# Transposed projections with the bias on ScalarE, conv taps dealt by step length, later attention slots, and squares and log-sigmoid moved in layer two

## Chip, cores and metric

The kernel runs on one core of one Trainium2 chip. The metric is the device time of one execution in microseconds (us), as the median of three.

## What is computed

Two transformer layers on 256 tokens of width 2048, all in float32. The first (biases and LayerNorm left out here where the change does not touch them):

```python
proj = x @ w_in + b_in              # 2048 -> 5376
c_val, c_glu, c_gate, q, k, v, a_gate = split(proj)   # 1024 x4, 128, 128, 1024
h = c_val * sigmoid(c_glu)
h = layer_norm(causal_depthwise_conv(h, width=31) + conv_b); y_conv = silu(h) * silu(c_gate)
y_attn = sliding_window_attention_with_sinks(q, k, v) * silu(a_gate)   # 16 heads of 64, 2 KV heads
x = layer_norm(ALPHA * x + concat(y_conv, y_attn) @ w_out + b_out)
```

The second layer mixes a sparse attention (NSA, 8 heads of 128) with a gated linear attention (GLA, 4 heads, values 256 wide), then has a cross attention and a gated feed-forward part:

```python
o_nsa = rms_norm(nsa(...), g_nsa_out)                  # RMS norm of each head's row
log_a = log_sigmoid(a_l @ w_gk2 + b_gk) / 16
o_gla = rms_norm(gla(q_l, k_l, v_l, log_a), g_gla_out) * silu(r_l)
x = x + concat(o_nsa, o_gla) @ w_out_2
```

## The kernel before

The time is set by weights passing through TensorE. All weight matrices are cut into 552 **weight steps** of 256 rows (two k-tiles of 128) by mostly 512 columns. A float32 product is made of three products in the rounded type fp32r: each operand is split into a high part and a low rest, and hi x hi, lo x hi and hi x lo are added up in PSUM. `gemm` (L347, L348, L349) does one step: for each of two k-tiles and each of two token tiles three matmuls, 12 in all, each with a 128x128 block of activations stationary (`aH`, `aL`) and 512 weight columns moving. A PSUM pair therefore holds tokens on its partitions and weight columns along the row.

Weights come in chunks of two steps. SP starts one DMA for each chunk into `raw` (4 buffers). ScalarE (ACT) casts raw to `hi` (L358), VectorE (DVE) subtracts to `lo` (L366), each three steps ahead of the step that TensorE (PE) works on. On DVE this is `keep_up(p)`: at the point p of its program it makes the `lo` of step p+3. So a DVE that is late with its other work makes PE wait for `lo`.

Order of the groups of layer one (steps): cv0 0-7 and cv1 16-23 (conv value), cg0 8-15 and cg1 24-31 (conv gate), q0 32-39, q1 40-47, kv 48-55 (256 columns), ga0 56-63, ga1 64-71 (gate of the conv branch), ag0 72-79, ag1 80-87 (gate of the attention), wo0 to wo3 88-119. Then layer two: ..., lq1 168, lar0 176, lk 184, lv0 192, lv1 200, lr1 208, lr2 216-223 (256 columns), w2o0 224, ... Two PSUM pairs alternate between groups.

The other work is written by hand between the steps of each engine. On DVE, after a group's last step, it is evacuated from PSUM with a bias added: `evac` (L1711) for cv and q, `evac_stage` (L1723) for the gates, `glu` (L1727) for the product. The convolution is 248 **taps** of 128x256 (L1746 the first of a channel tile, L1750 the rest), 4 or 5 to a step from p=20 on, each waiting for the tap four before it. Value, query and gate must lie with channels on partitions, so PE transposes them in 128x128 blocks: `conv_in_T` L756 (2x8), `q_T` L767 (2x8), `gate_T` L829 (4x4), and ACT copies them from PSUM.

Attention of layer one is 16 heads, u=0 to 15. With i counted from step 56, head u has its scores on PE (L789, L790) in slot `score_slot`, at i = 2 + 7u//4; DVE does its softmax there (L1759 to L1763), ACT its exponentials, PE transposes the probabilities three steps later (L798) and multiplies by v five steps later (L809 to L811), DVE normalises at six (L1768 to L1772). The conv's LayerNorm runs at i=20 to 29 among them.

In layer two, i is counted from step 168. Log-sigmoid (ACT: Abs, Exp, Ln, L1461 to L1465) runs at i=27, DVE's scans at 29. The GLA levels run at i=31 to 46 on DVE; among them DVE takes the squares of the NSA rows (L2190, L2191). In lr2, DVE multiplies the NSA rows by their inverse root (L2205), copies the GLA output from PSUM (L2211) and squares it (L1958, L1959); after the last step of lr2 PE transposes the result for w2o0.

Of the kernel before, what the change touches and what calls it, by code (L numbers as in the profile page):

```python
# [75 lines left out]
def stack_kernel(nc, a, out):  # L76
# [48 lines left out]
    for g in groups:  # L125
        for c in range(g["kt"] // CHUNK):
            src = g["w"].rearrange("(k p) n -> p k n", p=P)[
                :, g["k0"] + CHUNK * c:g["k0"] + CHUNK * (c + 1), g["col"]:g["col"] + g["n"]]
            chunks.append(dict(src=src, n=g["n"], k=CHUNK, step=g["s0"] + 2 * c, group=g))
            g.setdefault("c0", len(chunks) - 1)  # L130
# [11 lines left out]
    with ExitStack() as ctx:  # L142
# [36 lines left out]
        cols = const("cols", [P, 165])  # L179
# [49 lines left out]
        def wait_raw(e, chunk, later=None):  # L229
            turns = 0 if later is None else plus(later, 16 * later[1] // (CHUNK // STEP * NRAW))  # L230
            e.wait_ge(s_raw[chunk % NRAW], 16 * (chunk // NRAW + 1) + turns)
# [95 lines left out]

        def gemm(pe, g, j, opH, opL, before=None, later=None):
# [22 lines left out]

        def split_hi(act, s, later=None):
# [7 lines left out]
        def split_lo(dve, s, later=None):  # L360
# [3 lines left out]
            if s >= NSLOT:  # L364
# [4 lines left out]
        bias_groups = ["cv0", "cg0", "cv1", "cg1", "q0", "q1", "kv", "ga0", "ga1", "ag0", "ag1",  # L369
                       "wo0", "wo1", "wo2", "wo3"]  # L370
# [10 lines left out]
        c_h = put("c_h", 128, [P, TT, C])  # L381
# [19 lines left out]
        pe_rows = put("pe_rows", 112.5, [64, P])  # L401
# [6 lines left out]
        PEK, PEV = 101, 133  # L408
# [4 lines left out]
        N_PAR = 16 * (len(row_loads) + 2 + 1 + 1 + 1)  # L413
# [5 lines left out]
        s_ch = sem("conv_input_ready")  # L419
        s_cht = sem("conv_input_transposed")  # L420
        s_pad = sem("conv_input_padded")
        s_hT = sem("conv_input_T_ready")
# [11 lines left out]
        s_gat = sem("gate_transposed")  # L434
        s_gT = sem("gate_T_ready")
# [53 lines left out]
        sc8 = put("sc8", 128, [P, TT, GH, DV])  # L489
        mx2, den2 = st2[:, 0:32].rearrange("p (u t) -> p u t", t=2), st2[:, 32:64].rearrange("p (u t) -> p u t", t=2)  # L490
# [18 lines left out]
        sq_m = put("sq_m", 112, [P, D])  # L509
# [28 lines left out]
        s_ffs = sem("ffn_scale_ready")  # L538
        sq_f = put("sq_f", 136, [P, D])
# [45 lines left out]
        def _(sp):  # L585
            def load(c, src=None, later=None):
                ch = chunks[c]
                if c >= NRAW:
# [3 lines left out]
                    else:  # L592
                        sp.wait_ge(s_lo, old["step"] + 2 + plus_steps(later))
                sp.dma_start(raw[:, c % NRAW, :ch["k"] * ch["n"]].rearrange("p (k n) -> p k n", k=ch["k"]),
                             ch["src"] if src is None else src).then_inc(s_raw[c % NRAW], 16)

            for c, ch in enumerate(chunks[:G["fg0"]["c0"]]):
# [14 lines left out]
                if g is not None and g["name"] in bias_groups and c == (g["c0"] if g["i"] else 3):  # L612
                    i = bias_groups.index(g["name"])
                    if i >= 2 and i < 13:
                        evacuated(sp, G[bias_groups[i - 2]])
                    if i >= 13:
                        sp.wait_ge(bias_used, i - 12)
# [39 lines left out]
        def _(pool):  # L657
# [53 lines left out]
            pool.dma_start(pe_rows[32:64, :], a["pe_v_2"][0]).then_inc(s_par, 16)  # L711
            pool.dma_start(cw_rows[:, :], a["conv_w"][0]).then_inc(s_par, 16)
# [12 lines left out]
        score_slot = {2 + 7 * u // 4: u for u in range(HEADS)}  # L725
# [6 lines left out]
        def _(pe):  # L732
# [7 lines left out]
            def param_columns():  # L740
# [3 lines left out]
                pe.transpose(ps_m[2][:, NCOL:165], pe_rows[:, :], ident[0:64, 0:64]).then_inc(s_cols, 1)  # L744
# [5 lines left out]
            def conv_in_T(j):  # L750
                pe.wait_ge(s_ch, j + 1)
                for c in range(4):
                    if c % 2 == 0 and j == 1:
                        pe.wait_ge(s_hT, c // 2 + 1)
                    for t in range(TT):
                        last = pe.transpose(ps_m[c // 2][:, (c % 2) * T + t * P:(c % 2) * T + (t + 1) * P],  # L756
# [1621 lines left out]
```

## Time and profile before

| | |
|---|---|
| time, median of 3 (lowest, highest) | 1740.74 us (1738.15, 1749.26) |
| the profiled execution | 1737.17 us |
| its span, first to last instruction | 1735.1 us |
| mean granted TensorE clock | 0.988 |
| busy: PE, DVE, ACT | 1652.0 (95%), 1076.1 (62%), 776.1 us (45%) |
| weight loads into PE (overlap PE) | 1363.4 us (79%) |
| DMA | 301.40 MB, mean 174 GB/s |

The profile is of one execution; its time and its span differ by 2.07 us, which lies outside the first and last instruction. Busy times are of one engine over the whole span. The profiler gives a matmul a duration longer than the distance to the next one, since they are pipelined; what a matmul costs is the distance between starts. Rows of a timeline give a start, a duration, the engine, the line, the operation, output and inputs, sizes, a count, and in brackets the idle time before it and what ended it.

### The profile page before, as it was taken

How to read it: one execution, taken by the hardware profiler on the slowest of the kernel's cores; microseconds unless marked ns; L12 is line 12 of the kernel's file. 1: busy time of each engine (PE TensorE's matmuls, PEld its weight loads, DVE VectorE, ACT ScalarE, POOL GpSimd, SP SyncE). 2: the span in 40 equal slices, each digit the busy share in tenths (PEclk: the TensorE clock that was granted, in tenths of full speed). 3: DMA queues.
4: the chain of work that ended last, by engine and by line, in shares of the span. 5: the costliest groups of instructions: out<-in, count | busy, mean ns of one | idle time of the engine just before them, and what ended most of it. 6: DMA issues, size and time to landing. Idle time of an engine off the chain costs nothing.

```text
span 1735.1 us, 21788 instructions
## 1 busy us (share of the span) xinstructions
PE 1652.0 (95%) x7929; PEld 1363.4 (79%) x7929; DVE 1076.1 (62%) x1531; ACT 776.1 (45%) x1025; POOL 18.3 (1%) x46
## 2 busy tenths in 40 slices
PE   7999898998999998999998999999999999999998
PEld 6877677786767887787887788888878888888787
DVE  5699996667755666977556655545454445445453
ACT  4433455533534455434554464444433344444332
POOL 3000000000100000000000000000000000000000
PEclk9999999999999999999999999999999999999999
DMA  7664342564576453336554355555555555555553
GB/s 262 204 242 158 119 150 71 184 207 132 169 234 206 127 169 121 98 122 219 180 175 154 122 172 193 193 189 183 185 192 193 192 192 185 185 191 193 175 192 117
DMA packets 160284, 301.40 MB, mean 174 GB/s; under 512 B 5507, under 2 KB 24737, under 8 KB 159696
## 3 DMA queue, kind: packets, MB, share of 16 engines
q1 hardware_dynamic: 159520, 300.14, 52.1%
q8 instruction: 49, 0.80, 0.2%
q0 software_dynamic: 688, 0.23, 0.1%
q14 instruction: 27, 0.22, 0.0%
HBM read 298.26 MB, written 2.10 MB: 173 GB/s over the span
## 4 chain that ended last, share of the span: by engine, by line
PE 82%; DVE 11%; issue 3%; ACT 2%; DMA 1%; DVEq 0%; SPq 0%; ACTq 0%
PE ps_g L347 25%; PE ps_g L349 25%; PE ps_g L348 25%; DVE cT L1750 3%; DVE lo L366 3%; PE ps_m L279 2%; DMA raw<-in_w_in_dram 1%; ACT hi L358 1%; PE ps_m L1055 0%; PE ps_m L997 0%; PE ps_m L840 0%; PE ps_m L939 0%; PE ps_m L920 0%; PE ps_m L1005 0%; DVE sS L1759 0%
## 5 line engine op out<-in xcount | busy, mean ns | idle before, releaser
L366 DVE TENSOR_TENSOR lo<-raw,hi 128x1024 fp32r<-128x1024 f32 (+3 forms) x552 | 652.3, 1185 | 536.6 <-ACT hi L358 528.1
L358 ACT CAST hi<-raw 128x1024 fp32r<-128x1024 f32 (+3 forms) x552 | 562.3, 1021 | 778.5 <-PE ps_g L349 754.2
L347 PE MATMUL ps_g<-hi,aH 128*128 128x512 f32 (+3 forms) x1696 | 665.2, 392 | 15.2 <-DVE lo L366 10.1
L348 PE MATMUL ps_g<-lo,aH 128*128 128x512 f32 (+3 forms) x1696 | 651.1, 384 | 0.0
L349 PE MATMUL ps_g<-hi,aL 128*128 128x512 f32 (+3 forms) x1696 | 650.8, 384 | 0.0
L347 PEld LDWEIGHTS ps_g<-hi,aH 128*128 128x128 f32 x1696 | 323.8, 191 | 81.8 <-issue 21.8
L349 PEld LDWEIGHTS ps_g<-hi,aL 128*128 128x128 f32 x1696 | 323.1, 191 | 63.0
L348 PEld LDWEIGHTS ps_g<-lo,aH 128*128 128x128 f32 x1696 | 323.6, 191 | 58.4 <-issue 0.5
L347 PE MATMUL ps_g<-hi,guH 128*128 128x512 f32 x352 | 137.2, 390 | 0.0
L349 PE MATMUL ps_g<-hi,guL 128*128 128x512 f32 x352 | 137.0, 389 | 0.0
L348 PE MATMUL ps_g<-lo,guH 128*128 128x512 f32 x352 | 137.0, 389 | 0.0
L1750 DVE SCALAR_TENSOR_TENSOR cT<-hT,convw,cT 128x256 f32<-128x256 f32 x240 | 99.2, 472 | 0.0
L348 PEld LDWEIGHTS ps_g<-lo,guH 128*128 128x128 f32 x352 | 66.1, 188 | 13.7
L347 PEld LDWEIGHTS ps_g<-hi,guH 128*128 128x128 f32 x352 | 66.1, 188 | 13.7
L349 PEld LDWEIGHTS ps_g<-hi,guL 128*128 128x128 f32 x352 | 66.1, 188 | 13.5
L296 ACT ACTIVATE aH<-ps_m,cols 128x256 fp32r<-128x256 f32 x64 | 25.7, 475 | 24.1 <-PE ps_m L279 24.1
L313 DVE SCALAR_TENSOR_TENSOR aL<-ps_m,cols,aH 128x256 fp32r<-128x256 f32 x64 | 27.1, 477 | 10.9 <-ACT aH L296 10.9
L279 PE MATMUL ps_m<-ident,x 128*128 128x128 f32 x128 | 19.9, 292 | 13.1 <-DVE x L1919 7.1
L279 PEld LDWEIGHTS ps_m<-ident,x 128*128 128x128 f32 x128 | 16.5, 150 | 16.9 <-issue 14.2
L2239 DVE TENSOR_TENSOR x<-x,ps_g 128x512 f32<-128x512 f32 x32 | 20.5, 683 | 13.2 <-PE ps_g L349 13.2
L347 PE MATMUL ps_g<-hi,mH 128*128 128x512 f32 x64 | 26.2, 409 | 0.0
L347 PE MATMUL ps_g<-hi,ycH 128*128 128x512 f32 x64 | 25.1, 392 | 0.0
(365 smaller groups left out, 1112.4 us busy)
## 6 DMA issues: line engine op xcount, KB each, us to landing
raw<-in_w_gu_dram SPq DMA_DIRECT2D x88, 1024.0 KB, 5.0
raw<-in_w_in_dram SPq DMA_DIRECT2D x76, 1024.0 KB, 6.0
raw<-in_w_down_dram SPq DMA_DIRECT2D x44, 1024.0 KB, 5.0
raw<-in_w_out_dram SPq DMA_DIRECT2D x32, 1024.0 KB, 5.3
raw<-in_w_ck_dram SPq DMA_DIRECT2D x8, 1024.0 KB, 5.4
raw<-in_w_cv_dram SPq DMA_DIRECT2D x8, 1024.0 KB, 6.6
raw<-in_w_in_dram SPq DMA_DIRECT2D x12, 512.0 KB, 3.7
raw<-in_w_cq_dram SPq DMA_DIRECT2D x4, 1024.0 KB, 5.5
```

The lines of the kernel that those rows point to most:

```text
L279: last = pe.transpose(build_bank(name, u)[:, (2 * k + t) * P:(2 * k + t + 1) * P], src(2 * u + k, t), ident[:])
L296: last = act.activation(dst_k, src_k, ACT.Copy, scale=gain(2 * u + k))
L313: last = dve.scalar_tensor_tensor(out=dst_lo(2 * u + k, 1).rearrange("p k t -> p (k t)"), in0=bank[:, k * T:(k + 1) * T], scalar=gain(2 * ...
L347: pe.matmul(dst, xh, wh, start=first, stop=False)
L348: pe.matmul(dst, xh, wl, start=False, stop=False)
L349: last = pe.matmul(dst, xl, wh, start=False, stop=final)
L358: act.copy(step_view(hi, s), raw_view(s)).then_inc(s_hi, 1)
L366: dve.tensor_tensor(step_view(lo, s), raw_view(s), step_view(hi, s).bitcast(F32), ALU.subtract).then_inc(s_lo, 1)
L1750: dve.scalar_tensor_tensor(out=cT[:, ct, :], in0=src, scalar=w, in1=cT[:, ct, :], op0=ALU.mult, op1=ALU.add).then_inc(s_conv, 1)
L2239: dve.tensor_tensor(c, c, ps_g[pair_of(g)][t][:], ALU.add).then_inc(s_free[pair_of(g)], 1)
```

## The change

Layer one, products: the conv groups are now cm0 to cm3 (steps 0 to 31), each of 256 value and the matching 256 gate columns, loaded by two DMAs of 512 KB a chunk instead of one of 1024. For cm0-3, q0, q1, ga0, ga1 (64 steps) `gemm_T` makes the 128x128 block of weights stationary and 256 token columns of the activations move: 24 matmuls of 256 columns a step in place of 12 of 512. The result has channels on its partitions. The 48 transposes, their copies, `c_h`, and the bias evacuations on DVE of these groups go; ACT takes them from PSUM with a bias of one value for each partition (`columns`, `conv_gate`), and DVE makes the conv's input in two operations (`conv_input`).

Layer one, order: the taps go pair of tiles by pair, from p=9 on 4 a step and 3 at every fourth, 1 a step from p=46 to 55, then 5; the wait is for the tap two before. `k_T` and the slots of all 16 heads come one step later.

Layer two: log-sigmoid's three passes are at i=21, 23 and 26, the scans at 29 and 30. The squares of the NSA rows go from DVE to ACT (16 operations with a summed output, i=32 to 39), with the root at i=47. The squares of the GLA output go to ACT, straight from PSUM, in lr2. The evacuation of lr1 on DVE comes behind the scaling of the NSA rows, and the transposes of the first half of w2o0's input come inside lr2 at j=6, into buffers of their own (`y2H`, `y2L`).

```diff
-    for name, col, n in (("cv0", 0, 512), ("cg0", C, 512), ("cv1", 512, 512), ("cg1", C + 512, 512),
-                         ("q0", 3 * C, 512), ("q1", 3 * C + 512, 512), ("kv", 4 * C, 256),
+    for j in range(4):
+        group(f"cm{j}", w_in, T * j, NG)
+    for name, col, n in (("q0", 3 * C, 512), ("q1", 3 * C + 512, 512), ("kv", 4 * C, 256),
...
+                if "halves" in ch:
+                    for h in range(2):
+                        sp.dma_start(dst[:, :, h * T:(h + 1) * T], ch["halves"][h]).then_inc(s_raw[c % NRAW], 16)
...
+        def gemm_T(pe, g, j, before=None):
...
+            for k in range(STEP):
+                kk = STEP * j + k
+                first, final = kk == 0, kk == g["kt"] - 1
+                for ct in range(n // P):
+                    wh = step_view(hi, s)[:, k * n + ct * P:k * n + (ct + 1) * P]
+                    wl = step_view(lo, s)[:, k * n + ct * P:k * n + (ct + 1) * P]
+                    dst = ps_g[pair_of(g)][ct // 2][:, (ct % 2) * T:(ct % 2 + 1) * T]
+                    pe.matmul(dst, wh, aH[:, kk, :], start=first and ct % 2 == 0, stop=False)
+                    pe.matmul(dst, wh, aL[:, kk, :], start=False, stop=False)
+                    last = pe.matmul(dst, wl, aH[:, kk, :], start=False, stop=final and ct % 2 == 1)
...
-        score_slot = {2 + 7 * u // 4: u for u in range(HEADS)}
+        score_slot = {3 + 7 * u // 4: u for u in range(HEADS)}
...
-                    if g["name"] == "ga0" and j == 1:
+                    if g["name"] == "ga0" and j == 2:
                         k_T()
...
+            def columns(name, dst, func, b):
+                g = G[name]
+                psum_ready(act, g)
+                for ct in range(4):
+                    last = act.activation(dst(ct), ps_g[pair_of(g)][ct // 2][:, (ct % 2) * T:(ct % 2 + 1) * T], func,
+                                          bias=cols[:, b + ct:b + ct + 1])
...
+            def conv_input(j):
...
+                dve.wait_ge(s_stga, j + 1)
+                for c in range(2):
+                    ct = 2 * j + c
+                    dve.scalar_tensor_tensor(out=hT[:, ct, TAPS - 1:], in0=ps_g[pair_of(g)][0][:, c * T:(c + 1) * T],
+                                             scalar=cols[:, BCV + ct:BCV + ct + 1],
...
-                        dve.wait_ge(s_conv, i - 3)
+                        dve.wait_ge(s_conv, i - 1)
...
             def conv_share(p):
-                if p >= 20:
-                    conv(min(4 + p % 2, conv_units - conv_at[0]))
+                kv, rate = G["kv"]["s0"], 0
+                if 9 <= p < kv - 2:
+                    rate = 3 if p % 4 == 0 else 4
+                elif kv - 2 <= p < ga:
+                    rate = 1
+                elif p >= ga:
+                    rate = 5
+                conv(min(rate, conv_units - conv_at[0]))
...
-                    if i == 27:
-                        log_sigmoid()
+                    if i in (21, 23, 26):
+                        log_sigmoid((21, 23, 26).index(i))
+                    if 32 <= i < 40:
+                        nsa_squares(2 * (i - 32))
+                        nsa_squares(2 * (i - 32) + 1)
+                    if i == 47:
+                        root(ss_n)
...
+                    if g["name"] == "lr2" and 2 <= j <= 5:
+                        gla_squares(j - 2)
...
                 if i >= 2:
                     pe.wait_ge(s_goc, i - 1)
+                    pe.wait_ge(s_gsq, i - 1)
...
+                    if here == ("lr2", 6):
+                        build_pe(pe, "y2", y2_src, before_y2, only=range(0, 4))
```

How the instructions stand, first on DVE behind the evacuation of the group before q0's, from p=24 of the kernel before. L366 is one step's `lo`, L1711 the evacuation, L1750 the taps:

```order
L1750 SCALAR_TENSOR_TENSOR cT<-hT,convw,cT 128x256 x5
L366 TENSOR_TENSOR lo<-raw,hi 128x1024
L1711 TENSOR_TENSOR c_h<-ps_g,bias 128x512 x2
L1750 SCALAR_TENSOR_TENSOR cT<-hT,convw,cT 128x256 x4
L366 TENSOR_TENSOR lo<-raw,hi 128x1024
L1750 SCALAR_TENSOR_TENSOR cT<-hT,convw,cT 128x256 x5
```

In the changed kernel the taps begin behind cm0, from p=8 on (L399 is `lo`, L1740 the conv's input, L1761 and L1765 the taps):

```order
L1740 SCALAR_TENSOR_TENSOR hT<-ps_g,cols,stg 128x256 x2
L399 TENSOR_TENSOR lo<-raw,hi 128x1024
L1761 TENSOR_SCALAR cT<-hT,convw,cols 128x256 x2
L1765 SCALAR_TENSOR_TENSOR cT<-hT,convw,cT 128x256 x2
L399 TENSOR_TENSOR lo<-raw,hi 128x1024
L1765 SCALAR_TENSOR_TENSOR cT<-hT,convw,cT 128x256 x4
```

The taps moved 11 steps forward and each step has fewer of them; a pair of 512-wide evacuations became a pair 256 wide.

Second, DVE in lr2 of the kernel before. L1948 evacuates lr1 and lr2, L1905 and L2205 invert the root and scale the NSA rows, L2211 copies the GLA output:

```order
L2162 COPY sT<-ps_m 128x512
L1948 TENSOR_SCALAR rl<-ps_g,stat 128x512 x2
L1905 RECIPROCAL st_134<-st_134 128x16
L2205 TENSOR_TENSOR yn<-yn,st_134 128x2048
L366 TENSOR_TENSOR lo<-raw,hi 128x512 x3
L2211 COPY yg<-ps_m 128x512
...
L1958 TENSOR_TENSOR sc_138<-yg 128x2048
L1959 TENSOR_REDUCE stat<-sc_138 128x8
L1908 TENSOR_SCALAR stat<-stat 128x8
```

The same place in the changed kernel (L1904 and L2192 are root and scaling, L1947 the evacuation, L2204 the copy, L399 `lo`):

```order
L2161 COPY sT<-ps_m 128x512
L1904 RECIPROCAL st_133<-st_133 128x16
L2192 TENSOR_TENSOR yn<-yn,st_133 128x2048
L399 TENSOR_TENSOR lo<-raw,hi 128x512
L1947 TENSOR_SCALAR rl<-ps_g,stat 128x512 x2
L399 TENSOR_TENSOR lo<-raw,hi 128x512 x2
L2204 COPY yg<-ps_m 128x512
...
L2204 COPY yg<-ps_m 128x512
L1907 TENSOR_SCALAR stat<-stat 128x8
```

The root and the scaling moved ahead of the evacuation, one `lo` stands between them, and the two squaring instructions are gone from DVE.

## Rows read from the trace of the kernel before

**Rows 1.** The profile's chain of waits, by engine, shares of the span.
```profile
PE 82%; DVE 11%; issue 3%; ACT 2%; DMA 1%; DVEq 0%; SPq 0%; ACTq 0%
```
**Rows 2.** Windows: us; busy of PE, PEld, DVE, ACT, POOL; granted clock, DMA, GB/s.
```profile
104.99:155.34 50.35, 47.38 (x209) 38.69 (x208) 50.35 (x97) 18.44 (x21) 0.00 (x0) 0.97 0.50 175
155.34:172.50 17.16, 13.42 (x105) 12.51 (x104) 17.16 (x39) 7.75 (x11) 0.00 (x0) 1.00 0.61 214
172.50:262.11 89.61, 81.08 (x380) 62.05 (x380) 85.71 (x199) 46.79 (x91) 0.00 (x0) 0.96 0.42 142
262.11:325.07 62.96, 55.85 (x262) 44.35 (x261) 40.50 (x75) 35.64 (x65) 0.00 (x0) 0.95 0.28 96
...
696.25:757.76 61.51, 58.19 (x315) 49.14 (x314) 55.03 (x72) 23.68 (x25) 0.00 (x0) 1.00 0.33 103
757.76:784.15 26.39, 19.13 (x139) 17.79 (x138) 20.05 (x25) 13.65 (x22) 0.00 (x0) 0.98 0.39 139
```
**Rows 3.** PE timeline: matmuls of 512 columns, then of 256 (group kv).
```profile
41.52 0.39 PE L347 MATMUL ps_g<-hi,aH 128*128 128x512 f32 x1
...
60.11 0.39 PE L348 MATMUL ps_g<-lo,aH 128*128 128x512 f32 x1
...
155.34 0.28 PE L347 MATMUL ps_g<-hi,aH 128*128 128x256 f32 x1
...
159.53 0.28 PE L349 MATMUL ps_g<-hi,aL 128*128 128x256 f32 x1
```
**Rows 4.** DVE timeline: five taps and one `lo`.
```profile
102.09 2.05 DVE L1750 SCALAR_TENSOR_TENSOR cT<-hT,convw,cT 128x256 f32<-128x256 f32 x5
104.07 1.21 DVE L366 TENSOR_TENSOR lo<-raw,hi 128x1024 fp32r<-128x1024 f32 x1
105.21 1.26 DVE L1750 SCALAR_TENSOR_TENSOR cT<-hT,convw,cT 128x256 f32<-128x256 f32 x3
```
**Rows 5.** DMA issues of the first weights: KB each, us from issue to landing.
```profile
raw<-in_w_in_dram SPq DMA_DIRECT2D x76, 1024.0 KB, 6.0
...
raw<-in_w_in_dram SPq DMA_DIRECT2D x12, 512.0 KB, 3.7
```
**Rows 6.** PE timeline: the transposes of the conv's input in q0.
```profile
116.22 1.09 PE L756 MATMUL ps_m<-ident,c_h 128*128 128x128 f32 x8 [2.91 <-DVE c_h L1727]
```
**Rows 7.** DVE by line from 104.99 to 172.50: busy us, mean ns | idle.
```profile
L1711 DVE TENSOR_TENSOR q_sb<-ps_g,bias 128x512 f32<-128x512 f32 x4 | 2.5, 671 | 0.0
```
**Rows 8.** DVE timeline: the `lo` of steps 59 and 79.
```profile
180.10 1.21 DVE L366 TENSOR_TENSOR lo<-raw,hi 128x1024 fp32r<-128x1024 f32 x1
...
264.08 1.22 DVE L366 TENSOR_TENSOR lo<-raw,hi 128x1024 fp32r<-128x1024 f32 x1
```
**Rows 9.** PE timeline, ag0 and ag1: waits in attention.
```profile
278.73 0.41 PE L809 MATMUL ps_m<-v_sb,pT 128*128 128x64 f32 x2 [2.26 <-DVE q_sb L1772]
...
308.54 0.87 PE L798 MATMUL ps_m<-ident,sS 128*128 128x128 f32 x3 [2.60 <-ACT pT L1311]
```
**Rows 10.** PE timeline, lk and lv0: waits for the attention of layer two.
```profile
682.53 0.46 PE L1016 MATMUL ps_m<-vw,pT 128*128 128x128 f32 x2 [1.72 <-DVE yn L2085]
...
688.31 0.46 PE L1016 MATMUL ps_m<-vw,pT 128*128 128x128 f32 x2 [2.12 <-DVE yn L2085]
```
**Rows 11.** DVE timeline, GLA levels: squares of the NSA rows (first half).
```profile
714.03 1.21 DVE L2190 TENSOR_TENSOR stg<-yn 128x1024 f32<-128x1024 f32 x1
715.27 1.22 DVE L2191 TENSOR_REDUCE st<-stg 128x8 f32<-128x1024 f32 x1
```
**Rows 12.** Timelines of DVE and ACT in lr2.
```profile
763.71 0.25 DVE L1905 RECIPROCAL st<-st 128x16 f32<-128x16 f32 x1 [3.65 <-ACT st L1394]
...
777.59 2.29 DVE L1959 TENSOR_REDUCE stat<-sc 128x8 f32<-128x2048 f32 x1
...
760.09 1.49 ACT L1555 ACTIVATE rl<-rl 128x1536 f32<-128x1536 f32 x1 [0.96 <-DVE rl L1948]
```
**Rows 13.** PE timeline: the start of w2o0.
```profile
784.15 0.77 PE L347 MATMUL ps_g<-hi,aH 128*128 128x512 f32 x1 [4.13 <-issue]
```

More of the change, by code:

```diff
@@ L230, in wait_raw @@
             turns = 0 if later is None else plus(later, 16 * later[1] // (CHUNK // STEP * NRAW))
-            e.wait_ge(s_raw[chunk % NRAW], 16 * (chunk // NRAW + 1) + turns)
+            in_halves = sum("halves" in ch for ch in chunks[chunk % NRAW:chunk + 1:NRAW])
+            e.wait_ge(s_raw[chunk % NRAW], 16 * (chunk // NRAW + 1 + in_halves) + turns)
         def step_view(buf, s):
@@ L367, in split_lo @@
                               ALU.subtract).then_inc(s_lo, 1)
-        bias_groups = ["cv0", "cg0", "cv1", "cg1", "q0", "q1", "kv", "ga0", "ga1", "ag0", "ag1",
-                       "wo0", "wo1", "wo2", "wo3"]
+        bias_groups = ["kv", "ag0", "ag1", "wo0", "wo1", "wo2", "wo3"]
         bias_used = sem("output_bias_added")
@@ L1354, in _ @@
                         act.activation(rstd_sb[:], rstd_sb[:], ACT.Sqrt).then_inc(s_lna, 1)
-                    if i == 9:
-                        sigmoid(2, ACT.Silu)
-                    if i in (10, 11):
-                        gate_copy(i - 10)
+                    if i == 8:
+                        columns("ga0", lambda ct: gT[:, ct, :], ACT.Silu, BGA)
                     if i == LNI + 6:
@@ L1365, in _ @@
                         last.then_inc(s_lna, 1)
[L1366 to L1369 removed]
+                    if i == 16:
+                        columns("ga1", lambda ct: gT[:, 4 + ct, :], ACT.Silu, BGA + 4)
                     if i == 25:
[L1371 removed]
+                        silu_gate(0)
                     if i == LNI + 8:
@@ L1855, in _ @@
                 if i == 24:
-                    evac_stage(4, "ag0")
+                    evac_gate(0)
                 if i == LNI + 7:
-                    dve.wait_ge(s_gT, 4)
+                    evacuated(dve, G["ga0"])
+                    evacuated(dve, G["ga1"])
                     dve.wait_ge(s_lna, 3)
@@ L2206, in _ @@
                 [P, TT, QH, DK]), ALU.mult).then_inc(s_y2n, 1)
+            keep_up(G["lr2"]["s0"])
+            g = G["lr1"]
+            psum_ready(dve, g)
+            for t in range(TT):
+                take(g, t, rl[:, t, T:T + NG], 0, NG).then_inc(s_free[pair_of(g)], 1)
+            evacuated(dve, g)
             for i in range(4):
@@ L2225, in _, with y2_lo @@
                 [P, TT, GH, DV]), ALU.mult))
+            def y2_lo(us):
+                build_dve(dve, "y2", y2_hi_at, y2_lo_at,
+                          lambda k: cols[:, GNS:GNS + 1] if k < 8 else cols[:, GGL + k % 2:GGL + k % 2 + 1], only=us)
+            y2_lo(range(0, 4))
+            evac_rows("lr2", lambda t: rl[:, t, 768:])
             dve.wait_ge(s_rl, 1)
```

340 lines of the change are left out of this document (139 added, 201 removed).

## The prediction

> **What bounds the kernel now.** I read the chain of waits first, for which engine the end hangs on; then the windows, to see where TensorE is not the one; then the timelines of PE and DVE at the ends of those windows, for the waits themselves. The chain is 82% PE and 11% DVE [rows 1]: nearly everywhere the pace of matmuls is the time, and there is a stretch in which DVE is. The windows show it: from step 32 to 48 (104.99 to 155.34) and in kv (to 172.50) DVE is busy 50.35 of 50.35 and 17.16 of 17.16 us, PE 47.38 and 13.42 [rows 2]. In ga0 to ag0 (172.50 to 262.11) DVE has 85.71 of 89.61. In 262.11 to 325.07 DVE has only 40.50 of 62.96, yet PE lacks 7.1: there it waits for single results, not for load. The changed kernel can gain only in what PE lacks, and pays wherever PE's own work grows.
>
> The pace: 82 matmuls of 512 columns start between 41.52 and 60.11, 0.2267 us each; in kv 35 intervals take 4.19 us, 0.1197 each [rows 3]. So a plain step is 12 x 0.2268 = 2.72 us, and 24 of 256 columns are 24 x 0.1197 = 2.87. DVE's five taps take 104.07 - 102.09 = 1.98, so 0.396 each, and a `lo` 105.21 less 104.07, so 1.14 (its row shows 1.21 with the overlap) [rows 4]. With 4.5 taps a step DVE needs 1.14 + 1.78 = 2.92 in the before, more than PE's 2.72.
>
> **Terms, part by part** (against the profiled time of 1737.17; span 1735.1 and 2.07 around it).
>
> *Steps 0 to 31.* A step costs 2.87 - 2.72 = +0.15. 32 of them: +4.8. Stationary blocks are now weights, 24 loads a step against 12 before. That a load hides behind 256 columns is what kv shows: 104 loads, 12.51 us of busy time, 0.120 each, in 17.16 us, and the matmuls stay at 0.1197 [rows 2, 3]. The kv group has the same 24 loads a step, with activations in them; a weight block has the same size, so I take 0.1197, with 0 to +0.01 as bounds. The Trainium skill ("TensorE: Matmul & The Clock Gate", section "LDWEIGHTS (loading the stationary operand)") puts a load at the number of its columns over 1.2 ns, 107 ns for 128, an estimate just under the matmul's pace; by this rule the margin is a tenth, and the trace, with loads shown at 0.120, does not contradict it. The same page's "Back-to-back issue gap" gives a gap of N/2.4 + 2.5 ns, by which the 64 steps would cost 24 x 109.2 - 12 x 215.8 = 31 ns each, 2 us in all; the trace says 119.7 and 226.7, and 0.15 a step. The measurement decides.
> The first chunk comes as two DMAs of 512 KB: 3.7 us against 6.0 for one of 1024 [rows 5]; two in parallel share the engines, so I take +0.3 for the start (0 to +1). Later chunks are fetched eight steps ahead at a DMA share of 0.5 [rows 2], so nothing. One transposition block of conv_in goes, like the one at 116.22 with 1.09 us: about -0.9. DVE gets 3 or 4 taps a step, 3.75 on average: 1.14 + 1.49 = 2.63 below 2.87, plus two conv-input operations of tap size (0.8) once in eight steps; PE stays ahead. The tap's wait for the tap two before could stall it: a tap shows 0.41 us and starts 0.396 apart, so the one two before ended 0.38 us earlier; nothing (0 to +0.05 a tap, hidden by the 0.24 that is free). Sum at step 32: +4.2.
>
> *Steps 32 to 55.* They took 67.51 us, bound by DVE: 100% busy, with two evacuation pairs of q (4 x 0.671 less overlap, 2.5) and the gate's (1.2) and the product `glu` [rows 2, 7]. The new order leaves PE as the bound: 16 x 2.87 + 8 steps of kv at 24 x 0.1197/2 = 1.44, 11.5, together 57.5. The wait of 2.91 at L756 [rows 6] and a half-clock spell behind it go (clock 0.97 of 50.35 us: 1.5 us [rows 2]). -10.0, so step 56 begins 5.8 early (-3 to -7: DVE may still be a little late at kv, whose steps are 1.44 long while a `lo` of 0.6 and one tap of 0.4 fit, 1.0).
>
> *Steps 56 to 75.* From the `lo` of step 59 (180.10) to that of 79 (264.08) DVE needs 83.98 us for 20 turns of its program [rows 8]. The first started 7.6 us behind PE's step 56; at the nominal lead it would be 1.3 behind. Of the 6.3 us nothing is left if DVE is on time in kv. The load: 5 taps a step for 4.5, +9 taps, +3.6; four half evacuations of ga (4 x 0.67 less overlap) -2.4, and one softmax fewer before step 76, about -1.4. -0.2, so the stretch stays DVE-bound at about 84, and PE's +2.4 in ga0 and ga1 hides in it (16 x 2.87 + 4 x 2.72 and the attention's small matmuls are some 76). Some idle of DVE behind k_T's later slot, +0.5. Together -6.0 (-3 to -7).
>
> *Steps 76 to 87.* PE waits 2.26 us at L809, the same again 22 us later, and 2.60 at L798 [rows 9], 7.1 in all; the clock's 0.95 of 62.96 us means 3.1 us more at half speed [rows 2]. All three waits are heads whose DVE part stands behind a LayerNorm pass. A slot one step later moves them off those; they may fall on others. One score more comes in here, +0.9. I take -5 (0 to -9), by far the least certain term.
>
> *wo0.* The last head is one step later; its probabilities, its product and the transposes for wo0 come 1.8 later in a chain that PE may cover (0 to +3): +1.8.
>
> *lk and lv0.* The waits of 1.72 and 2.12 [rows 10] stand behind DVE's normalising, which waits for ACT, which was held by three log-sigmoid passes at i=27. Spread over three steps they cost each at most one cast's delay. -3.2 (-1 to -4).
>
> *GLA levels.* The squares take 1.21 + 1.22 us on DVE, twice, 4.9 us [rows 11], in a window where DVE has 55.03 of 61.51 and PE 58.19 [rows 2]. PE can win at most the 3.3 it lacks: -3.1 (-2 to -3.5). On ACT, busy 23.68 in the window, 16 small operations have room.
>
> *lr2 and the start of w2o0.* PE has 19.13 of 26.39 us [rows 2]. DVE waits 3.65 for ACT's root before it scales the NSA rows, because lr1's silu (1.49, behind a table load) stands before it; later it squares the GLA rows (2.29 for the sum, as much for the product) and PE stands still 4.13 before w2o0 [rows 12, 13]. Now the root is early, the squares are gone from DVE and the transposes are inside lr2. Against that, PE's GLA output now also waits for ACT's squares, which queue behind the silu, and behind ACT in turn the casts of steps 222 and on. Without all waits 7.3 us could go; I take -3.2 (0 to -6), nearer to the middle than to either end, since a new wait of the silu's length plus its table, some 2.8, is as likely as not.
>
> Sum: 4.2 - 10.0 - 6.0 - 5.0 + 1.8 - 3.2 - 3.1 - 3.2 = -24.5. The profiled execution would take 1712.7 us; the median shown is 3.57 above the profiled one, so **1716.2 us**.
>
> **Rivals.**
>
> *The waits come back elsewhere* (0.20). PE's single waits in attention and in lr2 are chains through three engines; a moved slot may meet another LayerNorm pass, and the new wait for ACT's squares may cost what the root's wait gave. For it: three waits at three different heads, none of which has the same cause. Against: DVE has 22 us free there. Then steps 76 to 87 and lr2 give 0, steps 56 to 75 give 3, lk 2 and the levels 2: -5.8 - 3 + 1.8 - 2 - 2 = -11, 1730 us.
>
> *All waits go* (0.10). -9 at steps 76 to 87, -6 at lr2, and wo0's +1.8 hidden: -24.5 - 4 - 2.8 - 1.8 = -33, 1708, and as low as 1704 if the clock falls nowhere.
>
> *The loads do not hide* (0.04), the case that ends slower. It is one mechanism: PE's loads of weight blocks in gemm_T. In 104.99 to 155.34 a load shows 38.69 / 208 = 0.186 us [rows 2]. If that were its own cost and not the pace of the matmuls beside it, a step of 24 loads would take 4.46 us in place of 2.87, +1.6; over the 48 steps 0 to 47 that is +76, and +18 in 56 to 75, where PE would pass DVE: about 1816 us. It decides for slower by over 1% (17.4 us) from +42 us on, which is 36 ns for each of 1152 matmuls, a pace of 0.156. The kv rows at 0.1197 with 24 loads a step speak against it plainly.
>
> **How the numbers follow.** Forecast 0.66, rivals 0.20, 0.10, 0.04. About 1% (17.4 us) is what a measurement of this kernel can tell from no change, so faster means below 1723.3, slower above 1758.1. The forecast's own terms add to a spread of some 8 us each way; nine tenths of it lie below 1723.3. With the second rival and none of the first: 0.60 + 0.10 + 0.04 for the first's lower edge = 0.74 faster. Same: the forecast's rest 0.06 and the first rival's 0.16 = 0.22. Slower 0.04. The range reaches down to 1704, the low end of the second rival, and up to 1731, just beyond the first.
>
> **What would show it.** In the changed profile: matmuls of gemm_T 0.120 apart; step 32 about 4 us later than 104.99 and step 56 near 166.7 in place of 172.50, with DVE below 100% between them; a clock of 1.00 in that stretch; the `lo` of step 79 near 252; PE waits of under 3 us in all in steps 76 to 87; w2o0's first matmul 20 to 25 us before 784.15, with PE's idle before it gone; nothing changed after it, since no instruction there moved. Wrong would be: matmuls of gemm_T further apart than 0.13; DVE still full to step 56 with PE waiting for `lo`; or in lr2 PE waiting at the GLA output for ACT as long as it waited before for DVE.

## The result

The changed kernel takes 1733.08 us in the median of 20 runs (1728.81 to 1738.43), the kernel before 1745.46 in 20 runs beside it (1737.07 to 1749.26; the three shown above had a median 4.7 lower). The ratio is 0.9935, interval 0.9922 to 0.9948: 11 us gained, where 24.5 were forecast. The forecast time lies 17 us off and the measured one outside its range. In the second comparison (below) the ratio is 0.9948 (0.9928 to 0.9969).

The profiled execution took 1735.88 us, and the one before 1737.17. This pair alone would say that nearly nothing happened, so it has to be read by stretches. The table gives, for stretches between the first matmuls of two steps, the change against before, in microseconds, raw and with the time lost to a halved clock taken out. That time is the sum over all microseconds of (1 - granted clock), from windows of 1 us: 20.5 us up to the last step in the profile before, 30.7 in that after.

| from step | to | forecast | raw | halved clock taken out |
|---|---|---|---|---|
| start | 32 | +4.2 | +4.5 | +4.5 |
| 32 | 56 | -10.0 | -9.9 | -8.2 |
| 56 | 76 | -6.0 | -6.3 | -4.6 |
| 76 | 88 | -5.0 | +4.0 | +4.0 |
| 88 | 96 | +1.8 | +1.2 | +1.2 |
| 96 | 192 | 0 | +8.2 | -2.0 |
| 192 | 200 | -3.2 | -3.0 | -3.0 |
| 200 | 216 | -3.1 | -3.0 | -3.0 |
| 216 | 232 | -3.2 | -0.6 | -0.6 |
| 232 | 551, the last | 0 | +3.3 | -0.1 |
| sum | | -24.5 | -1.6 | -11.9 |

The first row counts from the start of the trace; 0.4 us of it are a later first matmul. Taking the clock out is a little too kind where PE is not the bound: from step 96 to 120 both profiles take 74.5 us, though the changed kernel lost 1.1 us more there to the clock. The timed runs carry a granted clock too. Span times clock is 1701.5 us in the mean for the changed kernel and 1715.3 for the one before (27 runs, those beside e1 to e4 below), so -13.8; the mean clock is 0.983 against 0.985, which gives about 3 to 4 us back.

Windows of the profile after, steps 32 to 48, kv, 56 to 76, 76 to 84 and 84 to 88; columns as in [rows 2]:

```profile
109.48:155.56 46.08, 46.08 (x386) 46.08 (x385) 41.11 (x76) 17.73 (x22) 0.00 (x0) 1.00 0.57 195
155.56:167.08 11.52, 11.52 (x98) 11.52 (x97) 8.34 (x14) 7.62 (x12) 0.00 (x0) 1.00 0.76 269
167.08:250.43 83.35, 77.41 (x545) 69.23 (x543) 78.92 (x187) 45.09 (x92) 0.00 (x0) 0.98 0.43 140
250.43:292.23 41.80, 39.23 (x194) 30.81 (x193) 28.61 (x57) 22.87 (x40) 0.00 (x0) 1.00 0.21 70
292.23:317.41 25.18, 16.81 (x73) 13.12 (x72) 15.09 (x27) 15.82 (x29) 0.00 (x0) 0.86 0.35 129
```

The first two rows are what was forecast: PE full, DVE 41.11 of 46.08 where it was 50.35 of 50.35, clock 1.00, and 385 loads of weight blocks in 46.08 us, 0.1197 each, no more than the matmuls beside them. Kv is 11.52, forecast 11.5. The fifth row is where the expected gain went: four steps took 25.18 us, PE worked 16.81 of them, the clock was 0.86. The same four took 16.0 before.

PE's waits in those four steps, from the view of waits (in total, times, longest):

```profile
PE ps_m L812 <- ACT pT L1314: 6.6, 1, 6.6
PE ps_m L821 <- DVE q_sb L1787: 1.8, 1, 1.8
```

And who held it up, the timelines of ACT and then DVE (L1314 is the copy of the probabilities, L1353 the LayerNorm's silu, L391 the cast, L1304 the exponentials; L399 is `lo`, L1774 the start of a softmax):

```profile
291.16 1.28 ACT L1353 ACT_TABLE_LOAD   x1
292.45 4.05 ACT L1353 ACTIVATE cT<-cT,cols 128x256 f32<-128x256 f32 x8
296.41 1.97 ACT L391 CAST hi<-raw 128x1024 fp32r<-128x1024 f32 x2
298.40 1.28 ACT L1304 ACT_TABLE_LOAD   x1
300.11 0.40 ACT L1304 ACTIVATE sS<-sS,mx 128x128 f32<-128x128 f32 x1 [0.42 <-DVE mx L1778]
...
301.19 0.45 ACT L1314 COPY pT<-ps_m 128x384 f32<-128x384 f32 x1
...
297.47 1.22 DVE L399 TENSOR_TENSOR lo<-raw,hi 128x1024 fp32r<-128x1024 f32 x1 [6.79 <-ACT hi L391]
298.61 0.55 DVE L1774 SCALAR_TENSOR_TENSOR sS<-ps_m,mask 128x384 f32<-128x384 f32 x1
```

Read it backwards. PE wants, and at 301.79 begins, to transpose head 13's probabilities into a PSUM bank from which ACT must first copy head 12's. That copy (301.19) stands in ACT's program behind head 14's exponentials (300.11), these wait for head 14's softmax on DVE (298.61), that stands behind a `lo` (297.47) which waited 6.79 us for a cast, and the casts stand behind eight silus of the conv's LayerNorm (292.45 to 296.5). No engine is full; the order of three programs makes one chain of 10 us.

The same silus held up such a copy before the change too, at a lower price. The wait of 2.60 us at L798 in [rows 9] is this one. ACT in the kernel before (L1362 the silus, L1301 the exponentials, L1311 the copy):

```profile
300.57 4.04 ACT L1362 ACTIVATE cT<-cT,cols 128x256 f32<-128x256 f32 x8
...
306.86 0.40 ACT L1301 ACTIVATE sS<-sS,mx 128x128 f32<-128x128 f32 x1
...
307.94 0.46 ACT L1311 COPY pT<-ps_m 128x384 f32<-128x384 f32 x1
```

There DVE had finished the softmax (at 303.30) while the silus still ran. With the later slots the softmax itself stands behind the late `lo`, so the chain is longer.

In lr2, PE before w2o0 and DVE ahead of it (L2211 scales the GLA rows, L318 makes the low parts of w2o0's input, `y2`):

```profile
780.26 0.47 PE L358 MATMUL ps_g<-hi,y2H 128*128 128x512 f32 x1 [4.25 <-issue]
...
776.96 2.29 DVE L2211 TENSOR_TENSOR yg<-yg,stat 128x2048 f32<-128x2048 f32 x1
779.28 3.23 DVE L318 SCALAR_TENSOR_TENSOR y2L<-ps_m,cols,y2H 128x256 fp32r<-128x256 f32 x8
```

The wait of [rows 13] is as long as before, 4.25 us for 4.13. PE begins when y2's first low parts are there, and these stand behind a scaling that their matmuls don't need; the profile names no releaser ("issue"), and e7 below tests this.

### The profile page after: what moved, and what is told of

It is laid out like the page before. It is cut to its first block, busy times and chain, and to the rows that moved or that the text cites. A ratio compares the mean times of both kernels' runs of the same rounds, so it can differ in the third digit from the quotient of the medians.

```text
span 1733.9 us, 23281 instructions
## 1 busy us (share of the span) xinstructions
PE 1661.2 (96%) x8649; PEld 1406.2 (81%) x8649; DVE 1060.7 (61%) x1515; ACT 786.5 (45%) x1084; POOL 17.7 (1%) x47
## 4 chain that ended last, share of the span: by engine, by line
PE 86%; DVE 8%; ACT 2%; issue 2%; DMA 1%; DVEq 0%; SPq 0%; ACTq 0%
PE ps_g L358 23%; PE ps_g L360 23%; PE ps_g L359 23%; PE ps_g L380 3%; PE ps_g L382 3%; PE ps_g L381 3%; DVE lo L399 2%; PE ps_m L284 2%; DVE cT L1765 2%; ACT hi L391 1%; DMA raw<-in_w_in_dram 1%; PE ps_m L1046 1%; PE ps_m L988 0%; PE ps_m L841 0%; DVE sS L1774 0%
## 5 line engine op out<-in xcount | busy, mean ns | idle before, releaser
L399 DVE TENSOR_TENSOR lo<-raw,hi 128x1024 fp32r<-128x1024 f32 (+3 forms) x552 | 653.1, 1186 | 552.3 <-ACT hi L391 543.6
L391 ACT CAST hi<-raw 128x1024 fp32r<-128x1024 f32 (+3 forms) x552 | 562.8, 1021 | 760.8 <-PE ps_g L360 650.1
L358 PE MATMUL ps_g<-hi,aH 128*128 128x512 f32 (+3 forms) x1376 | 537.8, 391 | 1.5 <-issue 0.8
L359 PE MATMUL ps_g<-lo,aH 128*128 128x512 f32 (+3 forms) x1376 | 526.3, 382 | 0.0
L360 PE MATMUL ps_g<-hi,aL 128*128 128x512 f32 (+3 forms) x1376 | 526.1, 382 | 0.0
L358 PEld LDWEIGHTS ps_g<-hi,aH 128*128 128x128 f32 x1376 | 263.9, 192 | 53.5 <-issue 6.6
L380 PE MATMUL ps_g<-aH,hi 128*128 128x256 f32 x512 | 147.5, 288 | 3.8 <-DVE lo L399 3.8
L381 PE MATMUL ps_g<-aL,hi 128*128 128x256 f32 x512 | 145.8, 285 | 0.0
L382 PE MATMUL ps_g<-aH,lo 128*128 128x256 f32 x512 | 145.8, 285 | 0.0
L380 PEld LDWEIGHTS ps_g<-aH,hi 128*128 128x128 f32 x512 | 99.3, 194 | 5.2 <-issue 5.2
L1765 DVE SCALAR_TENSOR_TENSOR cT<-hT,convw,cT 128x256 f32<-128x256 f32 x240 | 100.6, 478 | 0.0
L381 PEld LDWEIGHTS ps_g<-aL,hi 128*128 128x128 f32 x512 | 99.3, 194 | 0.0
L382 PEld LDWEIGHTS ps_g<-aH,lo 128*128 128x128 f32 x512 | 99.1, 194 | 0.0
L359 PEld LDWEIGHTS ps_g<-lo,guH 128*128 128x128 f32 x352 | 66.1, 188 | 13.8
```

The costliest lines, as they stand in the source:

```text
L358: pe.matmul(dst, xh, wh, start=first, stop=False)
L359: pe.matmul(dst, xh, wl, start=False, stop=False)
L360: last = pe.matmul(dst, xl, wh, start=False, stop=final)
L380: pe.matmul(dst, wh, aH[:, kk, :], start=first and ct % 2 == 0, stop=False)
L381: pe.matmul(dst, wh, aL[:, kk, :], start=False, stop=False)
L382: last = pe.matmul(dst, wl, aH[:, kk, :], start=False, stop=final and ct % 2 == 1)
```

## The experiments

Times are medians, the ratio is against the kernel before on the same chip. The runs were made in three groups, each on a chip of its own (e1 to e4, e5 to e8, e9 to e11), so the groups are compared with one another and with the result by their ratios: a difference of 0.001 is 1.7 us. Lengths of stretches come from each run's profile, halved clock taken out unless said; times at which a step comes are as in the profile.

**e1, the slots back.**
```diff
-        score_slot = {3 + 7 * u // 4: u for u in range(HEADS)}
+        score_slot = {2 + 7 * u // 4: u for u in range(HEADS)}
```
(and `k_T` at j=1 again)

> The changed kernel with one part undone: the 16 heads' slots (and k_T) one step earlier, as before. In the changed kernel the stretch from step 84 to 88 takes 25.2 us where the kernel before takes 16.0, with PE waiting 6.6 us for a head's exponentials on ScalarE. Theory A (collision): with the later slots a head's exponentials come between the gate's silu at i=25 and the LayerNorm silu at i=26, so ScalarE loads its table four times instead of two and the casts wait behind; slots back to the old place take this away: steps 84 to 88 about 17 us, the time 5 to 8 us below the changed kernel, ratio to before about 0.989. Theory B (the waits come from PE arriving early, whatever the slots): steps 84 to 88 stay at 23 us or more, or the wait turns up two or three steps away, and the time is within 2 us of the changed kernel.

1730.98 us, ratio 0.9921 (0.9900 to 0.9943). Steps 84 to 88 fell from 21.8 to 14.6 us; raw 15.8, near the 17 expected. But by the ratios the time is only some 2 us below the changed kernel's, less than the intervals can tell and not the 5 to 8 expected, since steps 76 to 84 grew from 41.8 to 46.0. The waits from step 76 to 84 are those of the kernel before, 2.3 twice and 2.6:

```profile
PE ps_m L821 <- DVE q_sb L1787: 4.5, 2, 2.3
PE ps_m L812 <- ACT pT L1314: 2.6, 1, 2.6
```

So the collision belongs to the slots (Theory A), and its price was right, but A had missed that the late slots gain about 5 us ahead of it. Both signs are in the one edit.

**e2, the gate's silu beside the LayerNorm's**, to save table loads.
```diff
                     if i == LNI + 6:
+                        silu_gate(0)
...
-                    if i == 25:
-                        silu_gate(0)
```

> The changed kernel with ScalarE's silu of the first attention gate moved from i=25 to i=26, directly ahead of the LayerNorm silu and behind the head's exponentials. The slots stay late. Theory A (table loads on ScalarE): two loads of 1.28 go from the chain, steps 84 to 88 get 2.5 to 4 us shorter than the changed kernel's 25.2. If it is only the eight silu operations (4.05 us) that hold the casts up, not the tables, they stay within 1 us of 25.2. Theory B as for the run with the slots back: no change.

1733.41 us, ratio 0.9939 (0.9908 to 0.9969). Steps 84 to 88 took 22.6 us, 0.8 longer; PE's longest wait was 7.4. ACT where the two loads went:

```profile
291.12 0.40 ACT L1304 ACTIVATE sS<-sS,mx 128x128 f32<-128x128 f32 x1 [3.49 <-DVE mx L1777]
```

Counted from step 80, these exponentials begin 0.8 us earlier than in the changed kernel. The rest of the time that the two loads and the gate's silu took ahead of them is now spent standing still, waiting for DVE's softmax, and the gate's silu (1.06 us) stands in the chain behind them instead. So the two loads that e2 removes are worth 0.8 us, and not the wait of 6.6. Two more stand in the chain itself (at 291.16 and 298.40 in the changed kernel, 1.28 us each); what these cost no run tests.

**e3, the taps dealt as before.**
```diff
-                kv, rate = G["kv"]["s0"], 0
...
-                conv(min(rate, conv_units - conv_at[0]))
+                if p >= 20:
+                    conv(min(4 + p % 2, conv_units - conv_at[0]))
```

> The changed kernel with the conv taps dealt as before: none until p=20, then 4 and 5 in turn, also in the key and value group. Theory A (DVE's load by step length is what steps 56 to 76 gain from): DVE needs 2.92 us a step where PE needs 2.87, and in kv 2.4 where PE needs 1.44, so it enters step 56 some 7 us late; steps 32 to 56 take about 58 to 60 us, but steps 56 to 76 take 83 to 89 us less the taps already done, and step 76 comes 5 to 7 us later than in the changed kernel (250.4). Rival (the gain came from the evacuations and transposes that went, not from the dealing of taps): step 76 within 2 us of 250.4.

1737.88 us, ratio 0.9972 (0.9952 to 0.9992). Step 76 came 7.3 us later than in the changed kernel. The rows of 32 to 56 and 56 to 76:

```profile
109.23:170.96 61.73, 58.44 (x482) 57.74 (x481) 61.73 (x126) 26.35 (x35) 0.00 (x0) 1.00 0.58 196
170.96:257.77 86.81, 78.00 (x542) 69.55 (x543) 81.52 (x191) 44.29 (x92) 0.00 (x0) 0.98 0.43 140
```

DVE is full again to step 56, 61.73 of 61.73, and PE stands still 3.3 us. Step 56 comes 3.9 us later, and from there to step 76 another 3.5 are lost. Dealing is worth 6.0 us at step 96; that is Theory A.

**e4, layer one alone** (the edits of layer two left out).

> The kernel before with the change's first half only: transposed projections, taps and slots in layer one; layer two as before. My account of the two traces, with the time lost to a halved clock taken out of both, gives layer one -4.3 us at step 96 and layer two -7 us (lk to lv1 -6.1, lr2 -0.8). Theory A (the parts add up): ratio to before 0.996 to 0.999, that is -2 to -6 us, and against the changed kernel +6 to +8. Rival (the changed kernel's layer two gains only what the clock did not take, and in the median nothing): this kernel is as fast as the changed one within 2 us.

1737.84 us, ratio 0.9963 (0.9943 to 0.9982). Up to step 192 it is the changed kernel within 0.3 us. From 192 to 200 the changed kernel gains 2.9 us on it and from 200 to 208 another 3.0: log-sigmoid's and the squares' places, as forecast. In the profiles the parts add up. In the time layer two is worth 5 us by the ratios (0.9963 against 0.9935), a little under the 6 to 8 expected.

**e9, the dealing alone**, in the kernel before.
```diff
-                if p >= 20:
-                    conv(min(4 + p % 2, conv_units - conv_at[0]))
+                kv, rate = G["kv"]["s0"], 0
+                if 20 <= p < kv - 2:
+                    rate = 4 + p % 2
+                elif kv - 2 <= p < ga:
+                    rate = 1
+                elif p >= ga:
+                    rate = 6
+                conv(min(rate, conv_units - conv_at[0]))
```

> The kernel before with only the dealing of the taps: 4 and 5 in turn from p=20, one a step from p=46 to 55, then 6 a step to the end. Undoing the dealing in the changed kernel cost 5.8 us, as much as all of layer one had gained. Theory A (dealing and transposition need each other: only because the conv's input is there from p=9 can taps be taken out of kv without piling up behind it): step 56 comes 3 to 6 us earlier than in the kernel before (170.8 with the halved clock taken out), but 24 taps more stand behind it, 9.5 us of DVE, and step 76 comes 1 to 5 us later than before (257.0). Rival (the dealing is the gain by itself): step 76 comes 3 us or more earlier than before.

1753.52 us, ratio 1.0064 (1.0040 to 1.0089): slower. Against the kernel before, with the halved clock taken out, step 56 came 1.8 us earlier (less than the 3 to 6 expected), step 76 1.6 us later, and steps 76 to 80 lost 4.6 more. So dealing alone costs 6 us at step 96, and in the changed kernel, where e3 took it away, it gains 6 there: its sign depends on the rest. The rest of layer one without dealing (e3) costs 2.9 us against the kernel before, but that includes the late slots, which cost 3.2 at step 96 (e1); by this estimate transposition alone would be near zero. The comparison is not of one edit in two places: here the taps start at p=20 and go at 6 a step behind kv, there at p=9 and at 5. A likely reason for the two signs is that the transposed products bring the conv's input eleven steps earlier, so that taps taken out of the short steps of kv need not pile up behind it; no run moves that input alone.

**e5, late slots for heads 0 to 10, early ones for 11 to 15.**
```diff
-        score_slot = {3 + 7 * u // 4: u for u in range(HEADS)}
+        score_slot = {(3 if u < 11 else 2) + 7 * u // 4: u for u in range(HEADS)}
```

> The changed kernel with the late slots kept for heads 0 to 10 and the old, one step earlier slots for heads 11 to 15. The run with all slots back showed that the late slots gain 5.3 us up to step 84 (time at a halved clock taken out) and that the early ones save 7.4 us from step 84 to 88. Theory A (two effects of the slots at two places): this kernel has both; steps 56 to 84 within 2 us of the changed kernel's, steps 84 to 88 about 14 to 16 us, step 96 about 3 to 5 us before the changed kernel's, time 3 to 5 us below it. Rival (the gain before 84 is only time that PE had to give back anyway: an earlier PE finds the same ScalarE and DVE work of the LayerNorm in its way): step 96 within 1 us of the changed kernel's.

1726.19 us, ratio 0.9907 (0.9875 to 0.9938), by the ratios 5 us below the changed kernel, with 3 to 5 expected. Step 96 came 5.7 us earlier (0.8 of it is there at step 1 already, and not the slots' doing). Steps 84 to 88 took 14.7 us. Up to 84 a part of the late slots' gain is lost, 2.5 of about 5: one wait of 4.4 us at L821 stands in place of the others. Theory A holds, the rival falls.

**e6, head 12's copy ahead of the silus.**
```diff
-                if i - 4 in score_slot:
+                if i - 4 in score_slot and i != 28:
                     probs_copy(score_slot[i - 4])
...
                     if i == LNI + 6:
+                        probs_copy(score_slot[24])
```

> The changed kernel with one ScalarE copy moved: head 12's probabilities are copied from PSUM ahead of the LayerNorm's eight silus (i=26) in place of behind head 14's exponentials (i=28). TensorE transposes head 13 into the same PSUM bank and waits 6.6 us for that copy. Theory A1 (the bank and the place of the copy in ScalarE's order are the wait): the 6.6 us fall below 1.5; ScalarE stands still about 0.7 us for it; steps 84 to 88 take 4 to 6 us less than the changed kernel's 21.8 (halved clock taken out), unless the next wait in line (casts behind the silus, one `lo` late) takes some of it. Theory A2 (the casts and the softmax behind the eight silus set it): PE waits 3 us or more elsewhere in steps 84 to 88, and the stretch shrinks by less than 2.

1732.13 us, ratio 0.9937 (0.9918 to 0.9956), no faster than the changed kernel. The 6.6 us at L812 are gone, and steps 84 to 88 are 2.4 us shorter, not 4 to 6, because this came in their place:

```profile
PE ps_m L821 <- DVE q_sb L1788: 5.0, 2, 3.3
PE ps_m L803 <- DVE mx L1779: 1.4, 1, 1.4
```

The bank and the place of the copy made the wait (A1), and the casts behind the silus make most of it again (A2). The two stand one behind the other; taking one away gives back 2.4 of the 6.6 us.

**e7, y2's low parts first**; **e8**, that and e5 together; **e10**, e8 with the evacuation ahead of the scaling and the two scalings in one.
```diff
-            rooted(ss_g)
-            link(dve.tensor_tensor(yg[:], yg[:], ss_g.rearrange("p (t h) -> p t h", t=TT).unsqueeze(3).to_broadcast(
-                [P, TT, GH, DV]), ALU.mult))
...
             y2_lo(range(0, 4))
+            rooted(ss_g)
+            link(dve.tensor_tensor(yg[:], yg[:], ss_g.rearrange("p (t h) -> p t h", t=TT).unsqueeze(3).to_broadcast(
+                [P, TT, GH, DV]), ALU.mult))
             evac_rows("lr2", lambda t: rl[:, t, 768:])
```

> The changed kernel with two pieces of DVE's program swapped at the end of lr2: the low parts of w2o0's first operands (8 operations, L318) ahead of the scaling of the GLA rows (2.29 us, L2211). In the changed kernel w2o0's first matmul waits 4.2 us. Theory C (that wait is the scaling in front of the low parts, which is why lr2 gave 0.8 us and not 3.2): the first matmul comes 2.3 us earlier, and since DVE has 1 us to spare before the next transposes, 1.5 to 2.5 of it last to step 232. Rival (the wait belongs to the transposes or to ScalarE's high parts): under 0.5 us, or given back at step 226 when the scaled rows are wanted.

> The mixed slots and the swap at the end of lr2 together, as a candidate that beats both kernels. Both effects lie 400 us apart, so they add: 5 to 7 us below the changed kernel by Theory A and C, ratio to before 0.989 to 0.991; with the rival of either about 2 us less.

e7: 1728.93 us, ratio 0.9929 (0.9901 to 0.9957). w2o0 begins 2.5 us earlier, counted from step 222, and 2.2 are given back at step 226, the rival's place. PE's two waits and the DVE row behind the second:

```profile
771.62 0.47 PE L358 MATMUL ps_g<-hi,y2H 128*128 128x512 f32 x1 [1.70 <-issue]
781.76 1.06 PE L284 MATMUL ps_m<-ident,yg 128*128 128x128 f32 x8 [1.73 <-DVE yg L2220]
...
779.32 2.29 DVE L2220 TENSOR_TENSOR yg<-yg,rl 128x2048 f32<-128x2048 f32 x1 [2.11 <-ACT rl L1585]
```

DVE stood still 2.11 us for ACT's silu of lr2, because it had evacuated lr2 only behind the scaling. So the swap alone moved a wait. Yet the raw length of steps 216 to 232 is 50.2 us for 52.1: behind w2o0's start the clock did not halve, and that is 1.7 of the 1.9 us. In the time the ratio is 0.0006 below the changed kernel's, which the intervals can't tell from nothing. e8: 1723.42, ratio 0.9896 (0.9861 to 0.9930), by the ratios 7 us below the changed kernel, with 5 to 7 expected.

```diff
-            link(dve.tensor_tensor(yg[:], yg[:], ss_g.rearrange("p (t h) -> p t h", t=TT).unsqueeze(3).to_broadcast(
-                [P, TT, GH, DV]), ALU.mult))
...
             y2_lo(range(0, 4))
+            rooted(ss_g)
             evac_rows("lr2", lambda t: rl[:, t, 768:])
...
+            def scaled(h):
+                for t in range(TT):
+                    last = dve.scalar_tensor_tensor(out=yg[:, t, h, :], in0=yg[:, t, h, :],
+                                                    scalar=ss_g[:, 4 * t + h:4 * t + h + 1],
+                                                    in1=rl[:, t, h * DV:(h + 1) * DV], op0=ALU.mult, op1=ALU.mult)
+                return last
             dve.wait_ge(s_rl, 1)
...
+            for h in range(3):
+                scaled(h)
+            dve.wait_ge(s_rl, 2)
+            last = scaled(3)
...
```

> The kernel with mixed slots and the low parts first, with three things more at the end of lr2: DVE evacuates lr2 before it scales the GLA rows, and scaling by the root and by the gate are one operation for each head and token tile (8 of 256 columns, 0.4 us each) in place of two of 2.29; six of them need only the early part of the gate. In the run with the low parts first the 2.3 us gained at w2o0's start were given back at step 226, where TensorE waited 1.7 us for the gated rows, and DVE before that 2.1 us for ScalarE's silu behind the late evacuation. Theory C' (that is the whole of it): the gated rows are ready 2.5 to 3.5 us earlier, the wait at step 226 is under 0.3 us, and steps 216 to 232 take 46.2 to 46.8 us with the halved clock taken out, where the changed kernel and the last run take 48.5. Rival (the next thing in line, casts or the copies after the transposes, takes it): 48 or more.

e10: 1718.84 us (1716.90 to 1720.93), ratio 0.9874 (0.9835 to 0.9912). Its timeline of DVE:

```profile
768.15 0.88 DVE L1947 TENSOR_SCALAR rl<-ps_g,stat 128x256 f32<-128x256 f32 x2
769.07 3.26 DVE L2220 SCALAR_TENSOR_TENSOR yg<-yg,stat,rl 128x256 f32<-128x256 f32 x8
```

The gated rows are ready 6.6 us after w2o0's first matmul (765.76 to 772.33) where e7 needed 10.0; PE has no wait after w2o0's start, and steps 216 to 232 take 46.3 us without the halved clock. Theory C' as expected. This is the best version found: 26 us below the kernel before and 16 below the changed one, all three on one chip.

**e11, the changed kernel again.**

> The changed kernel itself, for a comparison with these candidates on the same chip: ratio to before 0.992 to 0.995. If a profile of its own shows the same lengths of all stretches but other places and another sum of halved clock, then the 10 us that the clock took more in its first profile are chance and not the change's doing: I expect 20 to 31 us lost by rows of granted clock, and lengths without it within 0.3 us from step 0 to 96.

1735.21 us, ratio 0.9948 (0.9928 to 0.9969), beside e10 on one chip. All stretches have the same lengths within 0.3 us up to step 96. But that the spells of halved clock would lie at other places did not come: 30.7 us were lost, as in the first profile, in twelve spells (before the last step) that each begin within 0.2 us of the first profile's. So these places are not scattered at random. They are not fixed either: the runs of the changed kernel have granted clocks from 0.979 to 0.987, by which one execution lost some 22 us and another 36 (an estimate, 1 - clock times the span), and the kernel before goes from 0.979 to 0.989.

## Why the prediction was wrong

*Steps 0 to 31 (+4.2)* came as +4.5: the pace of 256 columns was 0.1197 with weights stationary too, and the rival of loads that don't hide is dead by the loads of 0.1197 in the first window. (Its 1816 us is more than the terms that it names: 1716.2 + 76 + 18 is 1810.) *Steps 32 to 55 (-10.0)* was -9.9, *56 to 75 (-6.0)* -6.3, by the `lo` of step 79 at 250.80 for 264.08 [rows 8]; e3 shows its reason, DVE on time at step 56. Both are right in mechanism. In size, each has 1.7 us of halved clock that went; the prediction had counted 1.5 for the first and none for the second, so -6.3 for -6.0 is in part luck.

*Steps 76 to 87 (-5)* is the step that failed, by 9.0 us. As I put it: "A slot one step later moves them off those; they may fall on others." Up to step 84 the first half held, -5.1 raw, 2.0 of it halved clock. Then, from step 84 to 88, they fell on another: +9.2 raw, with a single wait of 6.6 us for ACT's copy. The sum for 76 to 87, +4.0, lies outside the bounds that I had given (0 to -9, none above zero): I had counted only the waits that could go. The working also had one of the three waits wrong. It took all three for heads "whose DVE part stands behind a LayerNorm pass", but the third, 2.60 us, is put down to ACT's copy in [rows 9]: it is the LayerNorm's silus on ACT, the same chain that cost 6.6 with the later slots. What stands on ACT between a head's exponentials and the next copy was in no term. The rival of returning waits had the mechanism, and not its size, for it too ended at 0 here. That its total of -11 us is what was measured is luck: it had -3 where -6.3 came and 0 where +4.0 came. Of the signs named ahead, the places of steps 32, 56 and 79 and the clock of 1.00 came; waits under 3 us in steps 76 to 87 and a w2o0 20 to 25 us earlier did not (8.4 us in steps 84 to 88 alone, and 3.9 us).

*wo0 (+1.8)* was +1.2. *lk and lv0 (-3.2)* and *the levels (-3.1)* were -3.0 each, told apart by e4.

*lr2 (-3.2)* was -0.6. The root's wait went, as forecast, and ACT's squares cost PE a wait of 2.0 at L1060, as feared. What I missed is that y2's low parts stay behind the scaling on DVE; e7 and e10 show that with the order changed the same stretch (steps 216 to 232, raw) gives 1.9 and 4.1 us more than it gave, 1.7 of it in each by the clock.

*The clock.* I had counted halved clock only as something to gain (1.5 us in steps 32 to 55, and 3.1 named in steps 76 to 87) and none as lost. The changed kernel has a mean clock of 0.983 in 20 runs and 0.982 in 10, the kernel before 0.985 in 27 and 16, so some 4 us go the other way. With the 9.0, the 2.6 and these the missing 13 us are more than covered. What the table's row from 96 to 192 gains (-2.0) is at least in part time in which a slow clock cost nothing.

The profile on which the sum was made was an unusually quick one of its kernel (1737.17 in a sample of median 1745.46, with a clock of 0.988). I took the median of three for the base, and that put the forecast and its range 5 us lower than its own sum deserved. With the base of 20 runs the measured time would lie inside that range; the gain would still be less than half of the one forecast.

Open: why the spells of halved clock in steps 96 to 168, whose code did not change, add up to 15.4 us in the changed kernel's two profiles and to 6.8 in the one of before. e4, which has the changed layer one alone, shows the same 15.4, and e3, with the taps dealt as before, 10.2; what in layer one moves them stays open.

## What to carry to other kernels

A slot moved by one step is not a wait taken away but a new meeting of three in-order programs: write down for each moved instruction what stands before it on its own engine, and bound the term above zero as well. An edit that loses by itself can gain beside another that makes room for it (e9 and e3, 6 us each way). Compare profiles step by step with the time of a halved clock put aside, then ask for the clock by itself, for it took back a quarter to a third of this gain.

## What the runs showed of the hardware

TensorE's granted clock fell to half, 1.2 GHz, at a stop of 4.1 to 4.3 us before w2o0's start, in all ten profiles that have one (4.13 us before, 4.25 after), and did not at one of 1.7 us, in all three (e7, e8, e10). The fall came during the stop or within 1 us of its end. The windows, one of the changed kernel after its stop and those of e7 and of e10 over all of w2o0 (step 224 to 232):

```profile
783.00:784.00 1.00, 1.00 (x3) 0.74 (x3) 0.29 (x1) 0.63 (x1) 0.00 (x0) 0.50 0.00 0
```

```profile
771.62:797.55 25.93, 24.12 (x112) 19.67 (x113) 20.40 (x27) 13.67 (x21) 0.00 (x0) 1.00 0.52 184
```

```profile
765.76:789.50 23.74, 23.74 (x112) 19.71 (x113) 19.27 (x33) 13.69 (x21) 0.00 (x0) 1.00 0.58 217
```

So here a wait of 4 us costs more than itself: e10 did w2o0 in 23.74 us, the changed kernel in 25.31 with a clock of 0.93 and no wait after the start. And the places of halved clock were the same, within 0.2 us, in two profiles of the changed kernel, while small changes of the program gave another sum: e10's profile lost 18.8 us in seven spells, the changed kernel's 30.7 in twelve.
